# Order of VectorE's work in the attention loop of two hybrid layers, and the places of its gate tiles

## What is computed

```python
scores = jnp.einsum('bnqhgd,bnkhd->bnhgqk', qb, kcat).astype(jnp.float32)
scores = scores * (HEAD_DIM ** -0.5)
scores = jnp.where(valid[None, :, None, None], scores, MASK_VALUE)
...
probs = jax.nn.softmax(jnp.concatenate([scores, sink], axis=-1), axis=-1)[..., :-1]
out = jnp.einsum('bnhgqk,bnkhd->bnqhgd', probs.astype(v.dtype), vcat)
...
gates = jax.nn.sigmoid(gate_logits).reshape(B, S, N_BRANCHES, D_MODEL)
merged = (gates[:, :, 0] * branch_a + gates[:, :, 1] * branch_b + gates[:, :, 2] * branch_c)
```

## Time and profile before

| | us |
|---|---|
| median of 3 runs | 2961.51 (2959.75 to 2961.97) |
| the profiled execution | 2960.76 |
| its span, first to last instruction | 2958.9 |
| TensorE busy | 2905.9 (98%) |
| ScalarE busy | 1596.6 (54%) |
| VectorE busy | 1061.7 (36%) |
| GpSimd busy | 412.4 (14%) |

### The profile page before, as it was taken

The page is one execution under the profiler, slowest core; times in us unless marked ns, Lnnn a source line. Parts: engine busy times, 40 slices in busy tenths (PEclk is TensorE's granted clock), DMA queues, the critical chain, the costliest instruction groups (busy, mean ns, idle before and its releaser), DMA issues.

```text
span 2958.9 us, 35240 instructions
## 1 busy us (share of the span) xinstructions
PE 2905.9 (98%) x13264; PEld 2372.4 (80%) x13264; DVE 1061.7 (36%) x2143; ACT 1596.6 (54%) x2318; POOL 412.4 (14%) x477
## 2 busy tenths in 40 slices
PE   8999999999999999999999999999999999999997
PEld 6889888888887668888887787788877788788885
DVE  4534436312113763121125214523244611542234
ACT  6655656554445765444455545645455644564555
POOL 1111111111111001111110111111111011111111
PEclk9999999999999999999999999999999999999998
DMA  8676767688898328898895697788878489788876
GB/s 241 145 152 133 169 130 157 142 195 193 192 196 178 86 43 182 192 193 194 194 196 117 145 194 173 187 186 197 183 186 187 87 179 195 158 197 192 201 182 161
DMA packets 138155, 503.81 MB, mean 170 GB/s; under 512 B 15473, under 2 KB 15729, under 8 KB 137873
## 3 DMA queue, kind: packets, MB, share of 16 engines
q0 software_dynamic: 68016, 248.22, 46.9%
q1 hardware_dynamic: 69120, 251.69, 28.5%
q10 hardware_dynamic: 864, 1.78, 0.2%
HBM read 499.53 MB, written 2.10 MB: 170 GB/s over the span
## 4 chain that ended last, share of the span: by engine, by line
PE 91%; ACT 3%; DVE 2%; issue 1%; DMA 1%; DVEq 0%; ACTq 0%; POOLq 0%; POOL 0%
PE ps L1019 74%; PE ps L1037 5%; PE ps L1359 3%; PE ps L1074 1%; PE ps L1131 1%; ACT arena L897 1%; PE ps L1300 1%; PE ps L1281 1%; PE ps L1282 1%; DMA wl<-weights 1%; PE ps L1114 0%; PE ps L1289 0%; ACT wl L450 0%; DVE arena L2185 0%; PE ps L1220 0%
## 5 line engine op out<-in xcount | busy, mean ns | idle before, releaser
L446 ACT ACTIVATE wh<-raw 128x1024 fp32r<-128x1024 f32 (+1 forms) x470 | 494.9, 1053 | 1050.4 <-PE ps L1019 976.6
L1019 PE MATMUL ps<-HH,wh 128*128 128x512 f32 x2224 | 873.3, 393 | 2.0 <-DVE HL L1537 1.2
L1019 PE MATMUL ps<-HH,wl 128*128 128x512 f32 x2224 | 865.6, 389 | 0.0
L1019 PE MATMUL ps<-HL,wh 128*128 128x512 f32 x2224 | 865.5, 389 | 0.0
L430 POOL DMA_DIRECT2D wl<-weights x470 | 410.5, 873 | 2541.3 <-ACT wl L450 2541.1
L1019 PEld LDWEIGHTS ps<-HH,wh 128*128 128x128 f32 x2224 | 417.5, 188 | 95.1 <-issue 7.9
L450 ACT ACTIVATE wl<-raw 128x1024 fp32r<-128x1024 f32 (+1 forms) x470 | 488.5, 1039 | 0.0
L1019 PEld LDWEIGHTS ps<-HL,wh 128*128 128x128 f32 x2224 | 417.6, 188 | 88.2 <-issue 3.1
L1019 PEld LDWEIGHTS ps<-HH,wl 128*128 128x128 f32 x2224 | 417.4, 188 | 87.3
L1019 PE MATMUL ps<-MH,wh 128*128 128x512 f32 x1056 | 411.9, 390 | 1.3 <-DVE ML L1940 0.7
L1019 PE MATMUL ps<-MH,wl 128*128 128x512 f32 x1056 | 411.0, 389 | 0.0
(11 more groups left out here) (306 smaller groups left out, 2899.5 us busy)
## 6 DMA issues: line engine op xcount, KB each, us to landing
raw<-weights SPq DMA_DIRECT2D x472, 512.0 KB, 6.1
wl<-weights POOLq DMA_DIRECT2D x470, 512.0 KB, 7.8
XT<-x SPq DMA_DIRECT2D x4, 512.0 KB, 6.7
out<-XT SPq DMA_DIRECT2D x4, 512.0 KB, 2.7
arena<-tables POOLq DMA_DIRECT2D x1, 1024.0 KB, 12.3
arena<-table_h ACTq DMA_DIRECT2D x1, 640.0 KB, 5.7
arena<-swaps_a POOLq DMA_DIRECT2D x1, 576.0 KB, 9.0
lpar<-layers ACTq DMA_DIRECT2D x2, 218.0 KB, 6.8
```

The source lines that it names most:

```text
L446: act_f(wh[:, n, 0:w], raw[:, n, 0:w], ACT.Copy)
L1019: op = mm(bank(g, t), w[:, slot, at:at + P], x[:, first + kt, :], start=(kt == 0 and w is wh and x is xh), stop=(kt == n_k - 1 and w is wl))
```

## The change

On VectorE, `softmax` is taken apart. `maximum(i)` makes the masked maximum and the bias of step i by themselves, with two drains of its own. Then comes `low_part(i-4)`, and then `normalise(i-1)`, sum, reciprocal and scaling of the step before, again with two drains. The negated maximum is now ahead of the sink's difference, which carries the signal to ScalarE. So the order in a turn is maximum, low part, sum of the other step, where it was low part, then both steps woven together.

On TensorE, 14 gate tiles stand ahead of the loop instead of 12, and the other 18 go in pairs into turns 0, 1, 2, 4, 7, 10, 13, 15 and 16; the other turns have none. ScalarE's second weight conversion of the loop stands in turns 8 and 9 instead of 9 and 10, since the gate tiles that free its slab end sooner.

```diff
-GATE_TILES, GATE_LEAD = 32, 12
+GATE_LEAD, GATE_AT = 14, (0, 1, 2, 4, 7, 10, 13, 15, 16)
...
-    return 2 if i in (0, 1, 2, H_STEPS - 1) else 1 if i < H_STEPS else 0
+    return 2 if i in GATE_AT else 0
...
-                    if i in (2, 9):
+                    if i in (2, 8):
                         high_part(s + (SLOTS + 1 if i == 2 else SLOTS + 2))
-                    if i in (3, 10):
+                    if i in (3, 9):
                         less_high_part(s + (SLOTS + 1 if i == 3 else SLOTS + 2))
...
+                def maximum(j):
+                    w, b = P if j % 4 == 0 else 2 * P, 16 + 8 * (j % 2)
+                    mx = col[:, 8 + 2 * (j % 2):10 + 2 * (j % 2)]
                     sink = lpar[:, L_SINK + 2 * (j // 4):L_SINK + 2 * (j // 4) + 2]
...
+                    for h in range(2):
+                        v.tensor_tensor_reduce(out=smH[:, j % 3, h * w:(h + 1) * w], in0=h_scores(gate, j, h, w),
+                                               in1=mask_h[:, 256 - w:256], scale=1.0, scalar=NEG, op0=ALU.add,
+                                               op1=ALU.max, accum_out=mx[:, h:h + 1])
                     dve.drain()
...
+                    v.scalar_tensor_tensor(out=mx, in0=mx, scalar=H_SCALE, in1=sink, op0=ALU.mult, op1=ALU.max)
                     dve.drain()
...
+                    v.tensor_scalar(col[:, b:b + 2], mx, -1.0, None, ALU.mult)
+                    v.tensor_tensor(col[:, b + 6:b + 8], sink, mx, ALU.subtract).then_inc(att_m, 1)
+
+                def normalise(j):
+                    w, b = P if j % 4 == 0 else 2 * P, 16 + 8 * (j % 2)
+                    den = col[:, b + 2:b + 4]
+                    v.tensor_tensor(den, den, col[:, b + 4:b + 6], ALU.add)
+                    dve.drain()
+                    v.reciprocal(den, den)
+                    dve.drain()
+                    for h in range(2):
+                        p = smH[:, j % 3, h * w:(h + 1) * w]
+                        op = v.tensor_scalar(p, p, den[:, h:h + 1], None, ALU.mult)
+                    op.then_inc(att_n, 1)
...
                 for i in range(H_STEPS + 4):
-                    if i >= 4:
-                        low_part(i - 4)
                     if i < H_STEPS:
                         dve.wait_ge(att_s, (a + i).value(1))
                         held(dve, dve_held)
...
+                        maximum(i)
+                    if i >= 4:
+                        low_part(i - 4)
+                    if 0 < i <= H_STEPS:
+                        dve.wait_ge(att_e, (a + i).value(0))
+                        normalise(i - 1)
```

More of the change, by code:

```diff
@@ L2191, in softmax @@
                     dve.drain()
[L2192 to L2195, removed]
+                    v.scalar_tensor_tensor(out=mx, in0=mx, scalar=H_SCALE, in1=sink, op0=ALU.mult, op1=ALU.max)
                     dve.drain()
-                    if here:
-                        v.tensor_tensor(col[:, b + 6:b + 8], sink, mx, ALU.subtract)
-                        v.tensor_scalar(col[:, b:b + 2], mx, -1.0, None, ALU.mult).then_inc(att_m, 1)
@@ L2227, in _ @@
                         held(dve, dve_held)
-                    if i <= H_STEPS:
-                        softmax(i, i < H_STEPS and (lambda h, w: h_scores(gate, i, h, w)),
-                                i > 0 and (lambda: dve.wait_ge(att_e, (a + i).value(0))))
+                        maximum(i)
[4 more added lines that the diff above has]
+                        normalise(i - 1)
                 def merged_low(s, first):
```

## The result

The changed kernel takes 2976.75 us, the median of 5 runs (2973.75 to 2978.95), against 2961.51 us for the one before. The ratio is 1.0051, with a 95% interval of 1.0039 to 1.0063: it is slower, by 15.2 us. Its profiled execution took 2974.56 us, 13.8 more than that of before.

A forecast was written before the change was run, and what follows sets the result against it. TensorE, at 98% of the span, was taken to bound the kernel, with VectorE and ScalarE pacing the loops. Terms -0.4 + 6.0 + 0.4 = 6.0 us a layer, 12.0 for two, gave 2972.8, median 2973.5; range 2964.5 to 2978.5.

The forecast's parts named there:

- the surplus above: Room at the upper end of the forecast range, up to 2978.5 us, for a wait the prediction had not seen.
- What bounds the loop before: Old attention loops: VectorE and ScalarE make the pace together, 2.99 us a step, while TensorE has slack.
- The new round: Loop chain score, maximum, low part, output, next score: 3.81 us a wide step, 35.84 us from score 5 to 15.
- Its pieces: Score to maximum 1.18 us, maximum to low part 1.23, low part to output 0.43, output to next score 0.97.
- rival 2: Same chain through the score but hand-overs 0.31 us a step shorter: 2967.3 to 2965.3 us; chance 0.12.
- Start and end: Loop's first steps 0.4 us sooner (0 to 1.4), from score 15 on 0.4 us later (-0.3 to 1.0).
- The second layer: Its attention loop was taken to repeat the first layer's, so 6.0 us a layer became 12.0 for two.
- Pairs at no cost and no gain: Gate tiles in pairs inside the loop, costed at nothing, since TensorE waits in each step anyway.
- The sum: Both loops: -0.4 + 6.0 + 0.4 = 6.0 us a layer, 12.0 for two.
- my case: Prediction's main outcome: slower attention loops, 2973.5 us, own bounds 2965.3 to 2976.7; chance 0.77.
- Rival 1: Low part does not gate TensorE; at 2.5 us a step 4.9 us a layer gained, 2951.7 us; chance 0.08.
- Rival 3: TensorE's clock falls in emptier steps, 1.8 us more a step: 2985 us, or 3009 over all; chance 0.03.

The follow-up runs named there:

- e7: Kernel before with only score i+1 moved ahead of output i-3 on TensorE: 2962.13 us, ratio 1.0004.
- e2: Kernel before with only the new places of the gate tiles and the weight conversion: 2961.78 us, ratio 1.0000.
- e3: Changed kernel with low part i-4 put back ahead of maximum i on VectorE: 2960.06 us, ratio to before 0.9993.
- e4: Changed kernel with score i+1 ahead of output i-3 on TensorE, from score 2 on: 2952.11 us, ratio to before 0.9965.
- e5: Changed kernel with an unused 128x512 copy on VectorE between maximum and low part, in each turn with a maximum: 2987.77 us, ratio 1.0085.
- e6: Changed kernel with an unused 128x512 copy on VectorE behind the low part, in each turn with a maximum: 2979.59 us, ratio 1.0061.
- e1: Changed kernel with gate tiles and weight conversion back at their old places, VectorE's new order kept: 2974.07 us, ratio to before 1.0042.
- e8: Changed kernel with score i+1 ahead of output i-3, gate tiles and conversion at their old places: 2953.27 us, ratio to before 0.9973.

## Why the prediction was right, and where it was off

The path that the prediction worked out is the one that the runs show. Two of its terms were too small, and that the median fell into the range is in part owed to the surplus above.

- **What bounds the loop before**, the hand-overs between VectorE and ScalarE at 2.99 us a step: right. e7 and e2 change TensorE's order and fill, and the time stays; e3 shortens VectorE's part of that round (the other step's sum is out of it) and the loop takes 28.93 us for 29.86.
- **The new round**: right, and shown three ways. Cut on VectorE (e3) or on TensorE (e4) it is gone; lengthened by 0.33 us (e5) each wide step is longer by 0.34; the same work beside it (e6) leaves the step as it was.
- **Its pieces**: score to maximum 1.22 us, put at 1.18; maximum to low part 1.24 (1608.82 to 1610.06), put at 1.23; low part to output 0.42, put at 0.43; output to score 0.97 as put. A wide step 3.85 for 3.81, one with a short output 3.40 (1615.31 to 1618.71) for 3.36, one with a short score 3.17 (1618.71 to 1621.88) for 3.13. The hand-over from the latent attention's rows was 0.04 us short, and this makes the 36.27 us out of 35.84. It also settles **rival 2**, which lived on a hand-over 0.31 us shorter.
- **Start and end**: from the first waiting score (score 2) to score 5 it was 9.15 us and is 8.88, so 0.3 sooner where I took 0.4. From score 15 to the next product 10.45 us for 9.97: 0.5 later where I took 0.4. I put that end down to low part 11 and to the pair in step 16; e1, which has VectorE's new order and no such pair, ends in 9.94 us, so it is the places of the gate tiles alone. The first loop has 6.6 us more than before, where I had 6.0.
- **The second layer**: I let it repeat the first. Its loop took 47.67 us in the trace of before (start of score 2, 2320.03, to start of output 15, 2367.70) and takes 54.99 (2325.08 to 2380.07), 7.3 more, while the first goes from 48.10 to 54.71. This term was mis-sized by 1.3 us: in the old order the second layer's loop was 0.4 us shorter than the first's, in the new one it is 0.3 longer. The 0.3 is one step: from score 8 to score 9 it is 3.45 us in the second layer (2345.08 to 2348.53) and 3.17 in the first, and the maximum of step 8 takes 0.71 us to its last accumulator read (2345.88 to 2346.59) where the first layer's takes 0.43. Both other traces of the changed kernel repeat this 3.45; what makes it is not shown. The earlier trace rows showed equal ends and not equal loops.
- **Pairs at no cost and no gain**: right inside the loop, by e1, whose ten steps take the same 36.27 us, and nothing shows in e2. At the loop's end they cost the 0.5 us a layer said above, which the sum had, in its term of 0.4. The cover of 2.84 us held: behind a pair, output 4 started 2.88 us after its score.
- **The sum**: 12.0 us forecast; 13.9 in the two loops of the trace, and 13.8 between the profiled executions, so what the rest of the kernel shifts nets to nothing (1.6 us sooner between the loops, 1.5 later behind them). The medians differ by 15.2, since the five runs lie on average above the profiled one. 2976.75 is in the range, above the 2973.5 forecast, by the 1.9 us of the terms above and by 1.4 us that lie between execution and median. It is at the very edge of the 2965.3 to 2976.7 us that my case's own bounds gave: the path was no luck, the closeness of the number in part was.
- **Rival 1**, a faster kernel, was wrong for this change but right on what the broken round would give once the low part does not hold up the next score: e4 is 10.6 us under before, where that rival had 9.8. The Trainium skill's rule (Perfetto Trace Analysis, section Optimization Strategy), to make what a gap waits for come sooner, was no bad advice by this; the order on the other engine had to go with it.
- **Rival 3**, the clock, did not happen in the three traces of the changed kernel. It is not as empty as I made it, though; see the last section. Its price of 1.8 us a step was too high, and it names no row for its 0.91 us of output: in a slow stretch of e5 an output and the score behind it took 0.74 and 0.68 us more than at 2.4 GHz, 1.4 in all.

## What to carry to other kernels

A wait that leads the table can be moved instead of closed: when work is moved ahead of a hand-over, follow what is queued behind the one who receives it, through every engine, until the path ends or comes back to its start. If it comes back, the sum of its pieces is the new time of a step, and it can be worked out beforehand from rows, here to 1% (3.81 for 3.85 us); what the change costs is a difference, and less exact (12.0 for 13.9 us). Here the round ran through an output that waited with the next score behind it; a product whose inputs are ready should not stand in the queue behind one that waits. Where no round runs through it the same move is worth nothing (e7).

## What the runs showed that I had not expected

TensorE's granted clock fell in some of these loops, for a few microseconds each time. The busy time by windows in e5's first loop (PE, PEld, DVE, ACT, POOL, then the granted clock and the DMA share), and the output and score that lie in the slow stretch:

```profile
1610.00:1615.00 5.00, 3.24 (x22) 2.74 (x20) 2.42 (x13) 2.34 (x8) 0.00 (x0) 1.00 0.83 192
1615.00:1620.00 5.00, 3.02 (x14) 2.65 (x12) 2.55 (x13) 1.85 (x7) 0.00 (x0) 0.73 0.02 3
1620.00:1625.00 5.00, 4.31 (x24) 3.34 (x23) 3.14 (x18) 2.14 (x8) 0.00 (x0) 0.92 0.01 2
1650.00:1655.00 5.00, 4.55 (x17) 3.84 (x18) 2.55 (x14) 1.27 (x6) 0.00 (x0) 0.66 0.01 2
```

```profile
1613.98 1.03 PE L1467 MATMUL ps<-arena 128*128 128x256 f32 x4
...
1617.21 1.92 PE L1489 MATMUL ps<-arena 128*128 128x128 f32 x8 [1.98 <-DVE ML L2214]
1618.92 1.91 PE L1467 MATMUL ps<-arena 128*128 128x256 f32 x4
```

After a stretch with TensorE 3.24 of 5 us busy the clock is 0.73 in the next five and 0.92 in the five behind it. Output 3 takes 1.71 us to the next score instead of 0.97, and score 7 1.35 us to the gate tile behind it (1618.92 to 1620.27), where the changed kernel's takes 0.67. Score 7 comes 4.94 us after score 6 where wide steps have 4.19, and score 8, at 1623.54, 4.62 us later where 3.40 + 0.33 were due: 1.6 us lost in all. Further on, from 1650, there is a second fall, and a third in the second loop (0.88 and 0.78 in the ten microseconds from 2385). e6 and e7 have one each in their loops:

```profile
1645.00:1650.00 5.00, 5.00 (x23) 4.07 (x22) 2.96 (x15) 0.70 (x3) 0.00 (x0) 0.66 0.00 0
```

```profile
2360.00:2365.00 5.00, 3.09 (x19) 2.51 (x17) 3.18 (x17) 3.59 (x11) 0.00 (x0) 0.84 0.00 0
```

In e6 it came around score 15, which is 4.20 us behind score 14 instead of 3.85, and the next product follows 11.76 us after score 15, where e6's second loop has 10.46: 1.7 us in all. e7 has it at the end of its second loop, which takes 13.02 us from score 15 to the next product, where its first takes 11.86: 1.2 us. The traces of before, of the changed kernel (three times), e1 to e4 and e8 have none in either loop. This is the mechanism of my third rival, in small: 1.2 to 1.7 us for each of the three falls that could be priced. A value between 0.5 and 1.00 is the mean of its two levels, 1.2 and 2.4 GHz, over a stretch. How empty the stretch before is does not settle it: the changed kernel has stretches with 2.67 of 5 us busy (1620 to 1625 us), emptier than the 3.24 in e5, and its clock stayed at 1.00. The Trainium skill (TensorE: Matmul & The Clock Gate, "A second HAM failure mode: psum-queue depth-cycling") tells of a clock that swings with many short gaps. These traces agree in kind, but in only 3 of 12, and not in the three of the changed kernel, which have a gap in nearly every step. e5's profiled execution, with three falls, was the longest of its four, at 2993.16 us. Whether such falls also make the longer executions of the changed kernel (2977.71 and 2978.95 us) is open: only executions up to 2975.09 us were traced.
